# A four-layer encoder kernel: the first two layers' phases against one woven stretch with context and main rows apart

## The reference, cut to what matters

```
m  = silu(c) @ w_mod[l] + b_mod[l]           # 9 vectors of 1024, for x and for z: 1024x9216 weights
x += 0.5*m2 * swiglu(modulate(rms_norm(x), m0, m1), ffn1_w1, ffn1_w3, ffn1_w2)   # 1024x2816, 2816x1024
z += the same with z's m
h  = modulate(rms_norm(.), m3, m4) @ w_in    # 1024x2336, x and z
mix = [2-D Fourier | neighborhood attention (x: window + context keys, bias) |
       bidirectional gated linear attention, x starting from z's final state |
       grouped-query attention with RoPE]    # 256 columns each
x += m5 * (mix_x @ w_out); x += 0.5*m8 * swiglu(modulate(rms_norm(x), m6, m7), ffn2_...)
z likewise, in layer 0 only (in layer 1, z gives keys, values and a state, and stops)
```

## Time and profile before

| | us |
|---|---|
| median of 3 runs (3763.21 to 3766.23) | 3763.43 |
| the profiled execution, its own time | 3768.65 |
| its span in the trace | 3766.9 |
| first block, 0 to 2593.7 in the trace | 2593.7 |
| second block | 1173.2 |

### The profile page before, as it was taken

How to read it: one execution, slowest core, us unless ns; L and a number is a source line. 1 busy time by engine, 2 the same in 40 slices (tenths; PEclk the granted TensorE clock), 3 DMA queues, 4 the chain that set the end, 5 groups by cost and what they waited for, 6 DMA issues and landing times. The chain is left out here.

```text
span 3766.9 us, 51231 instructions
## 1 busy us (share of the span) xinstructions
PE 3315.0 (88%) x20016; PEld 2872.0 (76%) x20016; DVE 1825.5 (48%) x2615; ACT 1359.8 (36%) x1902; POOL 205.5 (5%) x156
## 2 busy tenths in 40 slices
PE   6799979759979997699998758898989899998898
PEld 4588869546868885578887746798978898988797
DVE  5544452143344445644443143565465656465655
ACT  5422222113332224522223113434554444564343
POOL 0000010002000000000000010000011100011100
PEclk9999999755789998999999755999999999999899
DMA  8632212110123224833312110454434565433464
GB/s 287 196 110 98 91 52 69 52 22 1 45 68 100 90 88 159 265 101 100 100 67 76 53 22 12 135 194 137 139 118 130 163 201 175 147 106 120 151 195 141
DMA packets 368029, 430.76 MB, mean 114 GB/s; under 512 B 23364, under 2 KB 343668, under 8 KB 367604
## 3 DMA queue, kind: packets, MB, share of 16 engines
q1 hardware_dynamic: 367860, 428.41, 35.5%
HBM read 427.33 MB, written 1.05 MB: 114 GB/s over the span
## 5 line engine op out<-in xcount | busy, mean ns | idle before, releaser
L223 DVE TENSOR_TENSOR w_lo<-w_raw,w_hi 128x2048 fp32r<-128x2048 f32 (+1 forms) x224 | 505.9, 2274 | 523.6 <-ACT w_hi L216 523.6
L137 PE MATMUL psum<-xt_hi,w_hi 128*128 128x512 f32 (+1 forms) x1408 | 513.7, 365 | 14.8 <-PEq L327 14.8
L139 PE MATMUL psum<-xt_hi,w_lo 128*128 128x512 f32 (+1 forms) x1408 | 513.5, 365 | 0.0
L138 PE MATMUL psum<-xt_lo,w_hi 128*128 128x512 f32 (+1 forms) x1408 | 513.3, 365 | 0.0
L216 ACT ACTIVATE w_hi<-w_raw 128x2048 fp32r<-128x2048 f32 x232 | 434.6, 1890 | 61.4 <-PE psum L139 35.9
L1801 DVE TENSOR_TENSOR wl<-wr,wh 128x1024 fp32r<-128x1024 f32 (+3 forms) x336 | 381.6, 1176 | 71.6 <-ACT wh L1793 70.2
L1793 ACT ACTIVATE wh<-wr 128x1024 fp32r<-128x1024 f32 (+3 forms) x336 | 322.5, 996 | 110.7 <-DMA wr<-in_mlp_w_dram 76.9
L137 PEld LDWEIGHTS psum<-xt_hi,w_hi 128*128 128x128 f32 x1408 | 267.9, 190 | 57.5 <-issue 15.4
L138 PEld LDWEIGHTS psum<-xt_lo,w_hi 128*128 128x128 f32 x1408 | 268.0, 190 | 42.1
L139 PEld LDWEIGHTS psum<-xt_hi,w_lo 128*128 128x128 f32 x1408 | 267.6, 190 | 41.5
L694 ACT ACTIVATE gated_hi<-gated 128x512 fp32r<-128x512 f32 (+1 forms) x88 | 50.9, 579 | 680.1 <-DVE gated L751 680.1
(11 more groups left out here) (404 smaller groups left out, 6713.4 us busy)
## 6 DMA issues: line engine op xcount, KB each, us to landing
w_raw<-in_ffn_w_dram SPq DMA_DIRECT2D x132, 1024.0 KB, 5.4
w_raw<-in_w_mod_dram SPq DMA_DIRECT2D x72, 1024.0 KB, 5.1
wr<-in_mlp_w_dram SPq DMA_DIRECT2D x64, 1024.0 KB, 5.3
wr<-in_w_in_dram SPq DMA_DIRECT2D x56, 1024.0 KB, 5.1
w_raw<-in_w_in_dram SPq DMA_DIRECT2D x18, 1024.0 KB, 5.3
w_raw<-in_w_out_dram SPq DMA_DIRECT2D x8, 1024.0 KB, 7.7
wr<-in_mem_w_kv_dram SPq DMA_DIRECT2D x8, 1024.0 KB, 5.3
wr<-in_w_branch_dram SPq DMA_DIRECT2D x16, 512.0 KB, 3.4
```

What stands on the lines that cost most here:

```text
L137: pe.matmul(out, a[0], b[0], start=first, stop=False)
L138: pe.matmul(out, a[0], b[1], start=False, stop=False)
L139: return pe.matmul(out, a[1], b[0], start=False, stop=last)
L223: dve.tensor_tensor(self.w_lo[:, slot, 0:n], self.raw[:, slot, 0:n], self.w_hi[:, slot, 0:n].bitcast(F32), ALU.subtract).then_inc(self.spl ...
```

## The change

The first block becomes one list of pieces too (`Woven`, `Engine`), one chunk each: PE, ACT and DVE each walk it, and take side steps from two lines of stages, `urgent` first, then `background`. x and z become two streams with their own FFN, projection and mixers. Each weight matrix but `w_mod` is thus loaded and split once for each stream: 231 FFN chunks instead of 132, 48 projection chunks instead of 28, 72 modulation chunks as before. The ring has four chunks. Modulation pieces (`M0`, `M1`) are placed between FFN chunks. PSUM banks 6 and 7 take the pieces' results by turns, banks 0 to 3 the downward sums and the turns, banks 4 and 5 all mixer work; `held` keeps what the next user of bank 4 or 5 must wait for. Downward sums stay in PSUM for the whole FFN. `head_rms` scaling of the neighborhood queries and keys moves from DVE to POOL. There are no barriers between phases, and the second block is unchanged but for names.

```diff
+class Piece:
+    n_units, steps, fetch = 1, 4, ()
+    def act(self, act, step):
+        n = self.steps
+        for s in range(n // 2):
+            step()
+        self.early("act", act)
+        self.w.hi(act, self.m + 2, 0)
+        for s in range(n // 2, n):
+            step()
+        self.w.hi(act, self.m + 2, 1)
+        self.late("act", act)
+    def dve(self, dve, step):
...
+        self.w.lo(dve, self.m + 1, 0)
+        for s in range(n // 2, n):
+            step()
+        self.w.lo(dve, self.m + 1, 1)
+        self.late("dve", dve)
+class Engine:
+    def step(self):
+        for line in self.lines:
+            if line.advance():
+                return True
+        return False
+    def run(self):
+        for piece in w.pieces:
+            w.place[kind] = piece.m
+            for stage in piece.requires:
+                self.reach(stage, piece)      # takes steps until the stage is issued
...
+class ModulationPiece(Piece):
+    steps = 2
...
+    def pe(self, pe, step):
+        self.some(step, 0)
+        for h in range(2):
+            for k in range(KT):
+                last = pe.matmul(self.rows_bank(), b["silu"][:, k, :], wv[h][:, k, :], ...)
+        last.then_inc(w.used.sem, 1)
+        self.some(step, 1)
+        for i, q in enumerate(self.turns):    # two small matmuls each, rows into columns
...
+class SwiGlu:                                 # UpPiece: 48 matmuls of 256 columns
+        self.pieces = [self.up1[0], self.up3[0]]
+        for i in range(1, n):
+            self.pieces += [self.up1[i], self.down[i - 1], self.up3[i]] if i < n - 1 else ...
+class AffineTurn(Stage):                      # banks 0 to 3, or 4 and 5 with side=True
+        for k in range(KT):
+            back = 2 if self.side else 4
+            if k >= back:
+                pe.wait_ge(s.sem, s.at((k - back) // 2 + 1))
...
+class HeadAttention(Stage):                   # PE: three steps a unit
+            if u < n:
+                w.open(pe, 4)                 # waits for the Exp of unit u-1
+                last = pe.matmul(o, un["q"], k, start=True, stop=not biased)
...
+            yield
+            if u >= 1:
+                w.open(pe, 5)
+                pe.wait_ge(self.probs.sem, self.probs.at(u))
+                last = pe.transpose(w.ps[:, 5, i * P:(i + 1) * P], buf["p"][:, (u - 1) % 2, ...], w.eye)
+            yield
+            if u >= 1:
+                pe.wait_ge(self.moved.sem, self.moved.at(u))
+                last = pe.matmul(w.ps[:, 5, 0:HD], buf["pt"][:, i * P:(i + 1) * P], un["v"][i], ...)
+            yield
+    def act(self, act):                       # Exp of unit u, then the copy for unit u-1
...
+    order += M0[0:12]
+    urgent += [opening, sq_z, sq_x, After(w, M0[8]), z_t0, x_t0]
+    order += weave(zf1.pieces, M0[12:20], 3, 3)
+    tail = weave(xf1.pieces[3:], M0[20:36], 0, 2)
+    order += xf1.pieces[0:3] + z_in.pieces + tail
+    tail[0].fetch.append(zm.dft_in.fetch)
+    background += [After(w, z_in.last)] + zm.spectral() + zm.norms() + zm.decays(z_in.gt) + zm.gla_out()
+    background += [zm.st] + zm.head_turns() + zm.attention(None)
+    order += z_out.pieces
+    order += x_in.pieces
+    body = weave(zf2.pieces, M1[0:12], 1, 2)
+    body[0].fetch += [xm.dft_in.fetch, xm.gla_in.fetch]
+    cut = body.index(zf2.down[8])
+    order += body[:cut] + x_out.pieces + body[cut:]
+    order += xf2.pieces
+    order += M1[12:16]
+    xf3.pieces[0].after(x_t7)
+    order += weave(xf3.pieces, M1[16:24], 3, 3)
+    order += zf3.pieces[0:3] + x_in1.pieces + zf3.pieces[3:]
+    background += [After(w, x_in1.last)] + xm1.spectral() + xm1.norms() + xm1.decays(x_in1.gt) + xm1.head_turns()
+    order += M1[24:27]
+    order += zk.pieces                        # layer 1's context keys, values and state: 6 chunks
+    background += [After(w, zk.pieces[-1]), zk.decay, zk.na_norm, zk.gqa_norm, zk.state]
+    background += xm1.gla_out(zk.state.wait_done, ...) + [zk.na_turn, zk.g_turn]
+    background += xm1.attention(bias1, zk.na_turn.wait_done, zk.g_turn.wait_done)
+    for p_ in M1[27:32]:
+        p_.steps = 6
+    order += M1[27:32]
+    order += x_out1.pieces                    # its first piece is after the turn of the mixers' output
+    order += M1[32:36]
+    order += xf4.pieces
```

More of the change, by code:

```diff
@@ L257, in rows_of, with chunks_of @@
     return rows.rearrange("(k p) n -> p k n", p=P)
+def chunks_of(w2d, r0, nk, col0, ncols):
+    cw = min(CHUNK // nk, 512)
+    out, at = [], 0
+    while at < ncols:
+        out.append((w2d, r0, nk, col0 + at, min(cw, ncols - at)))
+        at += cw
+    return out
 class Chain:
@@ new lines, in split, with open, hold, claim @@
+    def split(self, pe, m):
+        pe.wait_ge(self.lows.sem, 2 * m + 2)
+        a, b = self.pieces[m].src.shape[1], self.pieces[m].src.shape[2]
+        return [t[m % RING][:, 0:a * b].rearrange("p (k n) -> p k n", n=b) for t in (self.high, self.low)]
+    def open(self, pe, bank):
+        for wait in self.held[bank]:
+            wait(pe)
+        self.held[bank] = []
+    def hold(self, bank, wait):
+        self.held[bank].append(wait)
+    def claim(self, pe, u):
+        if u >= 2:
+            pe.wait_ge(self.bank_free[u % 2].sem, u // 2)
+        return self.ps[:, 6 + u % 2, :]
@@ new lines, with __init__, __call__, blocked @@
+class Beat:
+    def __init__(self, step, groups, steps):
+        self.step, self.at = step, [j * groups // steps for j in range(steps)]
+        self.i = 0
+    def __call__(self):
+        for _ in range(self.at.count(self.i)):
+            self.step()
+        self.i += 1
+class Stage:
+    n_steps = 1
+    def __init__(self, w):
+        self.w, self.emitted = w, set()
+class After(Stage):
+    n_steps = 0
+    def __init__(self, w, piece):
+        super().__init__(w)
+        self.piece = piece
+    def blocked(self, kind):
+        return self.w.place[kind] <= self.piece.m
+    def pe(self, pe):
+        yield from self.hold("pe")
+    def act(self, act):
+        yield from self.hold("act")
+    def dve(self, dve):
+        yield from self.hold("dve")
+    def hold(self, kind):
+        while self.blocked(kind):
+            yield False
@@ L3103, in _, with __init__, fetch, wait @@
                 p_.pool(pool)
+class Loads:
+    def __init__(self, w, name, pairs, room=None):
+        self.w, self.pairs, self.room = w, pairs, room
+        self.landed = w.share(name, len(pairs), 16)
+    def fetch(self, sp):
+        if self.room:
+            self.room(sp)
+        with self.w.nc.allow_non_contiguous_dma(reason="small tables"):
+            for dst, src in self.pairs:
+                sp.dma_start(dst, src).then_inc(self.landed.sem, 16)
+    def wait(self, eng):
+        eng.wait_ge(self.landed.sem, self.landed.at(len(self.pairs)))
```

2887 lines of the change are left out of this document (1555 added, 1332 removed).

## The result

The change makes the kernel faster by 3.0%, less than forecast: 3653.36 us (median of 4 runs, 3650.78 to 3658.92) against 3764.83 (4 runs), ratio 0.9704 with a 95% interval of 0.9691 to 0.9717. The forecast was 3490, with 3390 to 3610 as its range. The profiled execution spans 3653.0 us; its first block ends at 2480.5, where 2319 had been summed. The second block is as long as before (1172.5 us against 1173.2), so the whole error is in the first.

What follows compares the result with a forecast made beforehand. First block bound by PE in about half its time, by transfers or latency otherwise; chunks, modulation, mixers, tail and turns summed to 2319 us instead of 2593.7, second block unchanged, giving 3490 us, range 3390 to 3610.

Steps and rivals of the forecast that it cites:

- rival (d): Doubled weight loads of the split streams add to the matmuls instead of hiding: 615 us, 4100 us in all; chance 1%.
- the tail: End of layer 1's mixers before `w_out`, mostly without weight chunks as cover: 160 us, units of 8.5 and 6.7 us.
- That ratio, 1.35, is one bound ... so I take 1.6: 220 us.: Mixers among weight chunks: cost over full-clock matmuls between 1.35 and 2.9, taken as 1.6, so 220 us for 138.
- With its other work DVE stays near 60%, so I charge nothing for the 119 more chunks.: First block's weight splitting: PE's matmuls hide DVE's extra splits, so no cost; uncovered, 2.5 us each, 300 us.
- rival (b): Side steps among chunks delay DVE's second half split, each holding PE 0.5 us more: 128 us, 3618; chance 26%.
- In layer 0 no window below 0.9 clock.: Expected sign in layer 0, where mixers run among weight chunks: PE's clock stays at 0.9 or above in every window.
- 172 us at half clock, 125 if the clock stays up. I take 160: End of layer 1's mixers: 122 us of attention units plus some 50 for the rest at half clock; 160 us charged.
- The three clusters: Modulation chunks `M1[12:16]`, `[24:27]`, `[32:36]`, 11 in all, each covering a residual, root and turn: 63 us together.
- (a): First block leaner, waits hidden as in the second block, with cheaper mixers, modulation and turns: 3366 us; chance 22%.
- (c): Doubled splitting on DVE and ACT sets the pace, 6.5 us a chunk instead of 5.7: slower than before; chance 2%.
- (e): Stages wait for one another, mixers end late and `w_out` waits in all three places: 3610 us; chance 7%.
- One announced sign of being wrong: FFN windows of the first block: the prediction is wrong if PE waits for transfers inside them.

Runs made afterwards that it cites:

- the fastest version: Changed kernel plus earlier Fourier tables, copy before exponential, tail transposes, split further ahead except in the opening, pause before gates, thinner third stretch: 3500.31 us, ratio 0.9296.
- the filled tail: Changed kernel with eight unused PE transposes ahead of each wait for copied probabilities in layer 1's attention: 3626.61 us, ratio 0.962.
- the copy first: Changed kernel with ACT copying unit u-1's transposed probabilities before the exponential of unit u in the attention: 3636.88 us, ratio 0.9651.
- Three edits that each removed a wait: Changed kernel with earlier Fourier tables, copy ahead of the exponential and eight filling transposes in layer 1's attention together: 3577.29 us, ratio 0.9493.

## Why the prediction missed

The direction held, and most terms did. The FFN's chunks, their doubling for two streams (rival (d) is out: the doubled weight loads stay hidden), the modulation between FFN chunks, the attention units of the tail (8.44 and 6.24 us against 8.5 and 6.7) and the second block came out as summed or a little cheaper. Four steps failed.

*"That ratio, 1.35, is one bound ... so I take 1.6: 220 us."* This is the term that was mis-sized: 347 us with the tables instead of 238, 109 of the 161 missed in the first block. The ratio came from rows of attention, and for attention it is right. It was laid on Fourier, norms, gates and levels too, which are chains of single small operations over three engines with one user of banks 4 and 5 at a time; those cost 2.7 times their matmuls. The full-clock work, too, was 159 us and not 138.

*"With its other work DVE stays near 60%, so I charge nothing for the 119 more chunks."* True where matmuls are alone (6 us for 33 chunks with 1.4 us more of DVE work in each), false in the packed stretches (48 us for 46 chunks). A mean share of 53% hides that DVE runs its list in order. The split is late whenever the step ahead of it waits, and with it the chunk. That is rival (b), which had a chance of 26%. The announced mark for it, 150 us of waits for `wl`, was passed (165.7), but only with the 34 us before the first mixer. With the split a chunk further ahead 41 us came back, so this mechanism is shown for about a quarter of the miss; the rest of these waits went over to the side steps themselves.

*"In layer 0 no window below 0.9 clock."* The 20 us around the first table wait had 0.74, and the first block lost 146 us at half clock, of which the forecast knew only the tail's, and that in part. The runs with waits put in show it by itself: a wait of 3.6 us cost 5.3, one of 1.07 us cost no clock. In the first parts of the mixers long waits (7.2, 6.5, 4.4) and dense short ones come together.

*The tail and the clusters.* "172 us at half clock, 125 if the clock stays up. I take 160": the clock did not stay up (0.67, then 0.50), and the tail took 180. The attention was right (129 us from 2095 to 2224, with the modulation chunks that still lie in it, against 122 for its units), and gates, state, outputs and turns of the keys took 45 us ahead of it and 6 behind, against some 50. These 51 hold one wait of 12.2 us (L1443) for a half split that DVE made after the root steps of two head norms. The five modulation chunks `M1[27:32]`, all within the 180, stood nowhere in the sum. The three clusters were 23 us over: in each PE waits 5 to 7 us for a split ahead of the turn and some 5 us behind it, and the clock falls beside both.

Of the rivals, (a), (c) and (d) are out, (e) did not occur (the mixers ended well before `w_out` in all places with cover), and (b) is the nearest, though its 3618 is still 35 us too low. The range's upper end, 3610, was half of (b) and (e), and neither had a term for the clock that is lost beside a wait (146 us in the first block).

What stays open: how the 232 us of the first parts divide between PE's early arrival, the bank shared by all steps and ACT's and DVE's order. The edits of the fastest version took 91 us off the three packed stretches together; the rest was not taken apart. That the fastest version comes to 3500 us, near the forecast, is no proof of the sum: two of its savings, the filled tail and the copy first, were never in it.

One announced sign of being wrong came true and is small: PE waited for a transfer inside an FFN, once, in the first:

```profile
129.48 2.00 ACT L251 ACTIVATE wh<-wr 128x1024 fp32r<-128x1024 f32 x2 [11.65 <-DMA wr<-in_ffn_w_dram]
132.98 0.58 PE L116 MATMUL psum<-zt_hi,wh 128*128 128x256 f32 x1 [7.93 <-DVE wl L259]
```

## What to carry to other kernels

When latency-bound work is put between matmuls, take the price of each kind of step from a row of that kind: attention units cost 1.6 times their matmuls here, chains of single operations 2.7. An engine that is half idle on average still delays others if a waiting step stands ahead of what they need, so put the work that feeds PE at least one whole piece further ahead than the step that can wait. Where PE must wait a microsecond or two in every short unit and the clock stays at half, harmless matmuls ahead of the waits can pay: 32 us here for 128 transposes.

## What was not expected of the hardware

- Half clock reaches beyond the wait: after 3.6 us without matmuls in full work the next ones ran at 1.2 GHz for 3.4 us (once 6.8), six times of six; after 1.07 us never, twelve times of twelve.
- In the tail PE was busy 77% of the time and the clock stayed at 0.50 for 99 us; with eight small transposes in each gap it was 0.85.
- Going from a weight matmul to a side step's costs PE little where it need not wait: at full clock in the first block 93 of 148 such places had the usual distance (0.12 or 0.23 us), nearly all others 0.1 us more. How the 63 us of step edges in the table come about is not shown.
- Three edits that each removed a wait added up fully (29 + 20 + 32 against 79 us), though two of them act on the same units.
